# Mixer layer of a transformer stack: state scan ahead of the pooling, output projection in another order

## The reference

```
h = rmsnorm(x, norm_mix) @ w_in                # 1024 channels: 512 for pooling, 512 for the state scan
# pooling half, 4 groups of 128 channels, windows w = 2, 4, 8, 16
d = trailing_mean(u_pool, w) - u_pool
y_pool = (d @ w_pool[group]) * pool_scale
# state half, 32 groups of 16 channels, 64 complex states each
s_t = A s_{t-1} + B u_t                        # diagonal, complex
y = gelu(Re(C s) + d_skip * u_ssm)
y_ssm = y * sigmoid(y @ w_glu + b_glu)
x = x + concat(y_pool, y_ssm) @ w_out
x = x + swiglu(rmsnorm(x, norm_ffn))           # then a last rmsnorm
```

## Time and profile before

| | us |
|---|---|
| median of 3 runs | 2361.54 (2360.8 to 2362.85) |
| the profiled execution, whole | 2362.24 |
| its span, first to last instruction | 2360.4 |
| PE busy in it | 2306.1 |
| mixer, `block_inputs(0)` to the first feed-forward product | 1857.6 to 1985.2 |

### The profile page before, as it was taken

The page is one execution under the profiler, slowest core; times in us unless marked ns, Lnnn a source line. Parts: engine busy times, 40 slices in busy tenths (PEclk is TensorE's granted clock), DMA queues, the critical chain, the costliest instruction groups (busy, mean ns, idle before and its releaser), DMA issues.

```text
span 2360.4 us, 32608 instructions
## 1 busy us (share of the span) xinstructions
PE 2306.1 (98%) x11768; PEld 1905.0 (81%) x11768; DVE 987.7 (42%) x1555; ACT 977.0 (41%) x1332; POOL 1152.2 (49%) x706
## 2 busy tenths in 40 slices
PE   8999999999999999999999999999999989999998
PEld 6888888878888887888888878888887767888886
DVE  5355353353444204553552342444376675222201
ACT  5444443244555314444443243555513435443321
POOL 3423334577995455333334464444455755444442
PEclk9999999999999999999999999999999999999999
DMA  5212223222233432222223323232333112333331
GB/s 196 87 62 87 78 71 105 92 86 97 89 91 106 133 98 78 64 86 78 79 74 94 98 81 98 89 107 89 107 104 111 45 40 87 99 97 98 98 98 54
DMA packets 61139, 214.17 MB, mean 91 GB/s; under 512 B 7184, under 2 KB 7440, under 8 KB 61072
## 3 DMA queue, kind: packets, MB, share of 16 engines
q1 hardware_dynamic: 58336, 205.11, 27.4%
q10 hardware_dynamic: 2736, 8.14, 1.1%
HBM read 211.13 MB, written 2.10 MB: 90 GB/s over the span
## 4 chain that ended last, share of the span: by engine, by line
PE 92%; DVE 4%; ACT 1%; POOL 1%; issue 1%; DMA 0%; SPq 0%; ACTq 0%; DVEq 0%; POOLq 0%
PE psum L803 88%; PE psum L920 1%; PE psum L907 1%; POOL xl L656 1%; DVE states L2182 1%; PE psum L886 1%; DMA convp<-in_convp 0%; PE psum L1183 0%; PE psum L972 0%; DVE pr L1822 0%; DVE states L2196 0%; ACT pt L1353 0%; PE psum L1009 0%; PE psum L896 0%; ACT r_tmp L1333 0%
## 5 line engine op out<-in xcount | busy, mean ns | idle before, releaser
L434 POOL TENSOR_TENSOR w_lo<-stage,w_hi 128x1024 fp32r<-128x1024 f32 x378 | 919.8, 2440 | 1118.7 <-ACT w_hi L1316 1104.0
L803 PE MATMUL psum<-xh,w_hi 128*128 128x512 f32 x1888 | 741.7, 393 | 15.7 <-DVE xl L2332 8.7
L803 PE MATMUL psum<-xl,w_hi 128*128 128x512 f32 x1888 | 736.6, 390 | 0.0
L803 PE MATMUL psum<-xh,w_lo 128*128 128x512 f32 x1888 | 736.4, 390 | 0.0
L1316 ACT ACTIVATE w_hi<-stage 128x1024 fp32r<-128x1024 f32 x377 | 396.6, 1052 | 354.4 <-PE psum L803 352.9
L803 PEld LDWEIGHTS psum<-xh,w_hi 128*128 128x128 f32 x1888 | 355.3, 188 | 98.4 <-issue 19.6
L803 PEld LDWEIGHTS psum<-xh,w_lo 128*128 128x128 f32 x1888 | 355.4, 188 | 75.0
L803 PEld LDWEIGHTS psum<-xl,w_hi 128*128 128x128 f32 x1888 | 355.6, 188 | 71.9
L803 PE MATMUL psum<-g_hi,w_hi 128*128 128x512 f32 x528 | 206.2, 391 | 0.0
L803 PE MATMUL psum<-g_hi,w_lo 128*128 128x512 f32 x528 | 205.4, 389 | 0.0
L803 PE MATMUL psum<-g_lo,w_hi 128*128 128x512 f32 x528 | 205.4, 389 | 0.0
(11 more groups left out here) (384 smaller groups left out, 3213.4 us busy)
## 6 DMA issues: line engine op xcount, KB each, us to landing
stage<-in_w SPq DMA_DIRECT2D x379, 512.0 KB, 3.5
bias<-in_bias ACTq DMA_DIRECT2D x8, 384.0 KB, 3.1
out_x<-out_t SPq DMA_DIRECT2D x4, 512.0 KB, 2.7
z<-in_x SPq DMA_DIRECT2D x3, 512.0 KB, 7.7
p_raw<-in_p ACTq DMA_DIRECT2D x2, 512.0 KB, 3.5
masks<-in_masks SPq DMA_DIRECT2D x1, 576.0 KB, 10.5
masks<-in_masks ACTq DMA_DIRECT2D x1, 576.0 KB, 4.5
stage<-in_w ACTq DMA_DIRECT2D x1, 512.0 KB, 5.1
```

Source lines behind the costliest of these rows:

```text
L434: pool.tensor_tensor(w_lo[s][:, :, :], stage[s][:, :, :], w_hi[s][:, :, :].bitcast(F32), ALU.subtract).then_inc(lo_done, 1)
L803: mm = pe.matmul(dst, lhs[i], rhs[j], start=start and n == 0, stop=stop and n == 2)
```

## The change

It reorders the mixer on all engines and adds one semaphore, `pool_scaled`. The matmuls and the element operations stay the same in number and shape.

- PE: `block_inputs(3)` comes straight behind in 6, in 7 moves behind `from_state(2)`. The gate comes next, then the state half of the output product, then the pooling half. The pool products stand between the units of the state half. Each has a PSUM bank of its own, the one from which `skip` has read.
- PE: `half_units`, which finished one result of 4 blocks after the other, is replaced by `half_pair`, which takes both banks, multiplies blocks 0 to 2 of the first and of the second result, then block 3 of each.
- POOL: all pooling waits until DVE has read the last block inputs, and runs with one weight unit's low part behind each group.
- ACT and DVE: pooling work behind the gate; ACT's `raw_out` of in 7 stands behind three `gelu_high`.
- SP: the weight units are loaded in the new order.

```
@@ POOL
             for u in range(4, 8):
                 mixer_low(u)
-            pooling(0)
             mixer_low(8)
-            pooling(1)
             mixer_low(9)
-            pooling(2)
-            mixer_low(10)
-            pooling(3)
-            for u in range(11, GU_U0):
+            pool.wait_ge(v_read, SP_T)
+            for g in range(SP_T):
+                pooling(g)
+                mixer_low(10 + g)
+            for u in range(10 + SP_T, GU_U0):
                 mixer_low(u)
@@ PE
                 def pool_product(g):
-                    dst = take_bank(MIX, WP_R0 + g)
                     if g == 0:
                         pe.wait_ge(wp_in, 16)
+                    pe.wait_ge(y_skip, g + 1)
                     pe.wait_ge(pooled, 2 * g + 2)
-                    pe.matmul(dst[:, :], w_pool[:, g, :], u_all[:, g, :], ...)
-                def half_units(u0, r0, count, ready, parts):
-                    for m in range(2 * count):
-                        u = u0 + m // 2
-                        if m % 2 == 0:
-                            take_unit(MIX, u)
-                        dst = take_bank(MIX, r0 + m)
-                        for k in range(SP_T):
+                    pe.matmul(Y[g][:, :], w_pool[:, g, :], u_all[:, g, :], ...)
+                def half_pair(u, r, ready, parts):
+                    take_unit(MIX, u)
+                    dst = [take_bank(MIX, r + h) for h in range(2)]
+                    for h, k in [(h, k) for h in range(2) for k in range(SP_T - 1)] + [(h, SP_T - 1) for h in range(2)]:
+                        if h == 0 or k < SP_T - 1:
                             pe.wait_ge(*ready(k))
-                            mm = passes(dst[:, :], wt(u, 4 * (m % 2) + k), ...)
-                        mm.then_inc(unit_used if m % 2 else mid_done, 1)
+                        mm = passes(dst[h][:, :], wt(u, 4 * h + k), ...)
+                        if k == SP_T - 1:
+                            mm.then_inc(unit_used if h else mid_done, 1)
...
                 in_unit(6, take_bank(MIX, MIN_R0 + 6))
+                block_inputs(3)
+                convolve(1)
                 from_state(0)
-                block_inputs(3)
-                in_unit(7, take_bank(MIX, MIN_R0 + 7))
-                convolve(1)
                 from_state(1)
-                pool_product(0)
-                pool_product(1)
                 convolve(2)
                 convolve(3)
-                pool_product(2)
-                pool_product(3)
                 from_state(2)
+                in_unit(7, take_bank(MIX, MIN_R0 + 7))
                 from_state(3)
-                half_units(MP_U0, MP_R0, 2, *pool_mix)
-                half_units(GLU_U0, GLU_R0, 2, *ssm_y)
-                half_units(MP2_U0, MP2_R0, 2, *pool_mix)
-                half_units(MS_U0, MS_R0, 4, *ssm_mix)
+                for i in range(2):
+                    half_pair(GLU_U0 + i, GLU_R0 + 2 * i, *ssm_y)
+                for i in range(4):
+                    half_pair(MS_U0 + i, MS_R0 + 2 * i, *ssm_mix)
+                    if i == 0:
+                        pool_product(0)
+                        pool_product(1)
+                    elif i < 3:
+                        pool_product(i + 1)
+                for i in range(4):
+                    half_pair(MP_U0 + i, MP_R0 + 2 * i, *pool_mix)
@@ ACT
-                pool_out(0)
-                pool_out(1)
-                gelu_high(0)
-                gelu_high(1)
-                pool_out(2)
-                pool_out(3)
-                gelu_high(2)
-                gelu_high(3)
+                for q in range(SP_T - 1):
+                    gelu_high(q)
+                raw_out(KT - 1)
+                ahead(KT)
+                gelu_high(SP_T - 1)
...
+                gate(0)
+                gate(1)
+                ahead(GLU_U0 + 1)
+                ssm_high(0)
+                gate(2)
+                ssm_high(1)
+                gate(3)
+                ssm_high(2)
+                ssm_high(3)
+                ahead(MS_U0)
+                ahead(MS_U0 + 1)
+                pool_out(0)
+                pool_out(1)
+                ahead(MS_U0 + 2)
+                pool_out(2)
+                ahead(MS_U0 + 3)
+                pool_out(3)
@@ DVE
+                skip(0)
+                skip(1)
+                yg_low(0)
+                skip(2)
+                yg_low(1)
+                yg_low(2)
+                skip(3)
+                yg_low(3)
+                gated(0)
+                gated(1)
+                mix_low(4)
+                gated(2)
+                mix_low(5)
+                gated(3)
+                mix_low(6)
+                mix_low(7)
+                ssm_half(0)
+                ssm_half(1)
+                mix_low(0)
+                mix_low(1)
...
                 for m in range(KT):
-                    if m >= 4:
-                        dve.wait_ge(bank_free[(MP2_R0 + m) % 2], free_before(MIX, MP2_R0 + m - 4) + 1)
-                    add_half(m, MS_R0 + m, MS_U0 + m // 2, MS_M0 + m // 2)
+                    dve.wait_ge(bank_free[(MS_R0 + m) % 2], free_before(MIX, MS_R0 + m) + 1)
+                    add_half(m, MP_R0 + m, MP_U0 + m // 2, MP_M0 + m // 2)
                     if m:
                         scaled_low(m - 1)
```

More of the change, by code:

```diff
@@ L402, in _ @@
             mix_u = DEPTH * LAYER_U
-            with sp.Fori(1, (mix_u + MP_U0) // RING) as n:
+            with sp.Fori(1, (mix_u + GLU_U0) // RING) as n:
                 for s in range(RING):
@@ L406, in _ @@
                     load(s, n * RING + s)
[L407 removed]
+            for u in range(GLU_U0, GU_U0 + 2):
                 s = u % RING
                 sp.wait_ge(lo_done, mix_u + u - RING + 1)
[L410 to L417 removed]
+                if u < MS_U0:
+                    load(s, mix_u + STREAM_GLU + u - GLU_U0)
+                elif u < MP_U0:
+                    load_halves(s, mix_u + STREAM_OUT + 2 * (u - MS_U0), 1)
+                elif u < GU_U0:
+                    load_halves(s, mix_u + STREAM_OUT + 2 * (u - MP_U0), 0)
                 else:
@@ L1579, in mixer, with gate @@
                 ahead(4)
-                for m in range(SP_T, KT):
+                for m in range(SP_T, KT - 1):
                     raw_out(m)
                     ahead(m + 1)
-                pool_out(0)
-                pool_out(1)
-                gelu_high(0)
-                gelu_high(1)
-                pool_out(2)
-                pool_out(3)
-                gelu_high(2)
-                gelu_high(3)
-                ahead(MP_U0 + 1)
-                for m in range(SP_T):
+                for q in range(SP_T - 1):
[3 more added lines that the diff above has]
+                gelu_high(SP_T - 1)
+                def gate(m):
                     if m % 2 == 0:
-                        ahead(GLU_U0 + m // 2)
                         act.wait_ge(mid_done, MIX * LAYER_M + (GLU_M0 + m // 2 + 1))
@@ L1601, in mixer, with ssm_high @@
                                    bias=mpar[:, BGLU_C + m:BGLU_C + m + 1]).then_inc(bank_free[m % 2], 1)
-                ahead(MP2_U0)
-                for m in range(SP_T):
+                def ssm_high(m):
                     act.wait_ge(y_ssm, m + 1)
                     act.activation(mix_hi[:, SP_T + m, :], u_all[:, SP_T + m, :], ACT.Copy).then_inc(mix_hi_s, 1)
-                ahead(MP2_U0 + 1)
+                gate(0)
[15 more added lines that the diff above has]
+                pool_out(3)
                 sqrt_table()
@@ L1609, in mixer @@
                     if m % 2 == 0:
-                        ahead(MS_U0 + m // 2)
-                    square(n0 + 1, m, sq_2, after(MS_R0 + m))
+                        ahead(MP_U0 + m // 2)
+                    square(n0 + 1, m, sq_2, after(MP_R0 + m))
                     act.activation(xh[:, m, :], z[:, m, :], ACT.Copy,
@@ L2241, in add_half, with gated @@
                     dve.tensor_tensor(z[:, m, :], z[:, m, :], U_BANK[r % 2][:, :], ALU.add).then_inc(bank_free[r % 2], 1)
-                def pool_half(m):
-                    if m < 4:
-                        add_half(m, MP_R0 + m, MP_U0 + m // 2, MP_M0 + m // 2)
-                    else:
-                        add_half(m, MP2_R0 + m - 4, MP2_U0 + m // 2 - 2, MP2_M0 + m // 2 - 2)
-                skip(0)
-                skip(1)
-                mix_low(0)
-                mix_low(1)
-                yg_low(0)
-                yg_low(1)
-                skip(2)
-                mix_low(2)
-                mix_low(3)
-                skip(3)
-                yg_low(2)
-                pool_half(0)
-                yg_low(3)
-                for m in range(1, 4):
-                    pool_half(m)
-                for m in range(SP_T):
+                def gated(m):
                     y = u_all[:, SP_T + m, :]
@@ L2267, in mixer, with ssm_half @@
                     dve.tensor_tensor(y, y, glu_sig[m % 2][:, :], ALU.mult).then_inc(y_ssm, 1)
```

(15 more changed lines are left out.)

24 lines of the change are left out of this document (13 added, 11 removed).

## The result

The changed kernel takes 2369.04 us (median of 9 runs, 2367.11 to 2371.24) against 2360.96 of the kernel before (9 runs, 2359.19 to 2362.85): 1.0031 times as long by the ratio of the runs, 95% interval 1.0023 to 1.0039. It is slower, by 8.1 us between the medians. The profiled execution is the quickest of the nine, 2367.11 us with a span of 2365.2, so its trace shows 4.8 of them (its span less that of the profile of the kernel before).

A forecast was written before the change was run, and what follows sets the result against it. PE was busy 98% of the span, so only its waits and low clock, at most 14 us, could be won. A feed-forward start at 1989.3 against 1985.2, less 0.6, made +3.5; clock 2.5 gave +6.0: 2367.5 us, range 2356 to 2374.

The forecast's parts named there:

- Step 1: State tiles without pooling: v_read of tile 3 at 1897.6 instead of 1910.8; PE's 7.0 us wait shrinks to 0.2.
- Step 2: Tile 3 beside pooling: its work behind v_read takes 15.5 us, so PE waits 3.2 us before from_state(3).
- check sum: Check from losses alone: 12.1 + 2.1 go, 21.9 come, leaving +6.7 with about 1 us of hand-overs left out.
- Step 3: Before the gate: in 7's bank is freed by raw_out 5.3 us after tile 3; PE waits another 3.3.
- Step 4: Both banks claimed at each unit's start: six of nine boundaries wait for read-out, 1.0 to 2.2 us each, sum 8.4.
- Step 5: DVE behind the gate: mix_low operations for state unit 0 are held up by POOL's work, costing 4.0 us.
- Step 6: The rest: loads stay hidden, PE's work from gate to first feed-forward product is 58.1 us, the 0.6 sum-of-squares wait goes.
- Step 7: Clock: a low level caused by two waits of some 3.3 us, 1.9 us apart, costs 2.5 us.
- second rival: Only DVE's delay by POOL behind the gate fails to come, saving 4.0 us: 2363.5 us, chance 0.22.
- first rival: POOL stands back for DVE's back-to-back operations, so from_state(3) meets no wait: 2354.6 us, chance 0.17.

The follow-up runs named there:

- experiment 5: The changed kernel, but ACT copies the result of in 7 before the three gelu pairs: 2369.29 us, ratio 1.004.
- experiment 1: The changed kernel run again, unaltered, beside the kernel before: 2369.64 us, ratio 1.0038.
- experiment 6: The changed kernel with pooling waiting for tile 3's scans, 2359.29 us, or for its two operations before the scans, 2368.57 us.
- experiment 4: The changed kernel, but POOL's pooling waits for the states of tile 3 instead of the reading of its block inputs: 2360.01 us, ratio 0.9997.
- experiment 7: The changed kernel with late second bank and pooling behind tile 3's states, 2354.78 us; also each result finished first, 2354.10; the latter with pooling behind scans, 2353.52.

## Why the prediction was right, point by point

The direction and the size held: +6.0 was forecast and +8.1 measured, 2369.0 in a range of 2356 to 2374. The mechanisms held too, but that the sum came so near is in part luck, as the table shows. The steps, each against the first trace of the changed kernel (steps 4 and 5 in the forecast's own measure, as distance from one matmul's start to the next beyond the usual 0.23 us; the view of waits counts each about 0.16 us less, from the listed end of the matmul):

| step | forecast | measured |
|---|---|---|
| 1: v_read of tile 3 (same origin) | 1896.9 | 1895.1 |
| 2: tile 3 behind v_read; wait before from_state(3) | 15.5; 3.2 | 15.6; 0.35 |
| 3: end of tile 3 to the gate; PE's wait | 5.3; 3.3 | 6.5; 4.4 |
| 4: six unit boundaries | 8.4 | 8.8 (view: 7.9) |
| 5: waits for `mix_lo` in state unit 0 | 4.0 | 1.6 (view: 1.3; again: 1.9) |
| 6: PE's own work from the gate to the feed-forward product | 58.1 | 59.7 |
| 7: low clock | 2.5 | 2.3 |

Step 1 came out better than forecast, as I had both low parts hold DVE; they stood back. (For the forecast the origin is moved by 0.7, since block_inputs(0) starts at 1856.9 here.)

Step 2's duration held, between the right rows (that of tile 3 before was 13.6 us behind v_read, 1910.8 to 1924.4, where the prediction reads 13.0; nothing in its sum uses it), but its wait was mis-sized: tile 3 began 1.8 us earlier, and PE came 1.1 us later to from_state(3), by the hand-overs that the check sum had noted.

Step 3's mechanism held, and its size was 1.2 us too small. yg_low(0) met POOL and took 1.72 us instead of 0.68, and skip(2), on which the third gelu waits, is queued behind it on DVE. What the step did not see is that its wait was not worth its length: experiment 5 took 2.5 us of it away and nothing was gained.

Step 4's mechanism is shown from both sides, by taking the wait out (-7.7, with step 3's share in it) and by putting it into the kernel before (+10.8). A boundary as the trace has it:

```profile
1924.83 0.39 PE L801 MATMUL psum<-yg_hi,w_lo 128*128 128x512 f32 x1
1926.20 0.47 PE L801 MATMUL psum<-yg_hi,w_hi 128*128 128x512 f32 x1 [0.98 <-ACT glu_sig L1597]
```

From start to start it is 1.37 us, 1.14 over the usual distance. The six are 1.14, 1.55, 1.14, 1.21 and, with scaled_low, 1.97 and 1.79.

Step 5 was over-sized by more than half in this trace and about right in experiment 5 (4.2). It depends on how far PE runs ahead of DVE. This was the second rival's condition, half met, and the time did not go to its 2363.5.

Step 6 held in that no wait on a transfer shows and the wait for the sum of squares is gone. But its 58.1 was 1.6 us too small (72.8 from the gate to the feed-forward product, less 8.8, 1.6, 0.4 for bank 0 and 2.3 for the clock): the third and fourth pool products took 1.15 us each instead of 0.92, and the first matmul behind each wait is some 0.1 us slower. This makes up for most of what step 5 had too much, and step 3's 1.2 for most of step 1's 1.8. That is the luck in the sum.

Step 7: the low level came with the size forecast, but inside one wait of 4.4 us and not behind two of 3.3. That it may come twice was not foreseen. This trace has +4.8 where +6.0 was forecast; that the median is +8.1, on the other side of it, is what experiment 1 shows: the second low stretch, and a profile of the kernel before that lay over its median.

The first rival, POOL standing back, was not what happened in tile 3, but it was no freak of one row: it happened in tiles 0 and 1, and experiment 6 brings it about on purpose. Its gain was priced too high: with tile 3 in 7.4 us it gave 2354.6, and experiments 4 and 6 measured 2360.0 and 2359.3. Had I asked where in a tile L744 of the earlier trace rows had asked, the row would have pointed to the cure.

## What to carry to other kernels

An alternating pair of result banks is worth its second bank only if it is taken as late as it is first written; a helper that claims both at its start turns each hidden read-out into a wait of about 1 us or more, and six of them were as large as the whole loss of this change. A loss can have two causes each as large as itself, when the change also brings a gain; that mending one of them restores the time does not clear the other. When work moves off a contended engine pair to start "as soon as possible", test a start some microseconds later: here the later start brought 9.6 us and cost one wait of 1.1. And price a wait by what the next consumer does with the time, since a wait in front of a late producer can be shortened for nothing.

## What the runs showed of the hardware

- The kept-out instruction. A POOL tensor_tensor that had stood idle and asked during DVE's six back-to-back two-input operations waited for all of them: 4.66 us instead of 1.29, 4.78 and 4.81 instead of 2.4. The same POOL instruction, asking during the first of the two operations before the scans or at the scans, was in within about 0.4 us (1.66 and 1.33 us in all), and from then on the two engines took turns, among the six too (L758 in experiment 6). The Trainium skill (SBUF — State Buffer, on the two separate sides) has the pair held for one instruction by whoever starts first, and the loser blocked. The turns agree with it; being kept out for up to six instructions is more than it says. Why the six kept POOL out and the operations before them did not is open.
- Scans take part in it: eight scans took 2.6 us alone and 3.8 and 4.8 beside POOL.
- The four DVE operations of a state tile that read PSUM ran 0.60 us apart beside POOL too, as in tiles 2 and 3 of the kernel before (1894.83 to 1897.23, 1908.32 to 1910.72).
- The low clock level (1.2 GHz) began inside or just behind waits of PE: inside the one of 4.4 us in the first trace of the changed kernel, 0.6 us behind the same wait in experiment 1, and there again inside one of 1.5 us that followed one of 1.4; it stayed for some 3.5 or 7 us each time. In experiment 4 and in 6 behind the scans, with six boundary waits of 1.0 to 1.8 us spread over the mixer, it did not come there. In the three kernels of experiment 7 it came for 3.6 us in two, behind waits of about 1 us for `mix_lo`, and not in the third, whose waits were nearly the same. I can't tell from these traces what decides.
